# Eight experts of a mixture layer: plain fp32 products on four column groups in place of high and low parts

## What is computed

```python
def moe_swiglu(h, w_router, b_router, w_gate, w_up, w_down):
    logits = (ht @ w_router) + b_router                  # 256 x 8
    top_val, top_idx = lax.top_k(logits, TOP_K)          # 2 of 8
    gates = jax.nn.softmax(top_val, axis=-1)
    combine = jnp.sum(jax.nn.one_hot(top_idx, N_EXPERTS) * gates[..., None], axis=1)
    for e in range(N_EXPERTS):
        y = y + combine[:, e:e + 1] * swiglu(ht, w_gate[e], w_up[e], w_down[e])
```

## Time and profile before

| what | value |
|---|---|
| median of 3 runs | 1327.01 us |
| span of the profiled execution | 1322.7 us |
| around the span (median less span) | 4.3 us |
| PE busy | 1273.1 us, 96% |
| PEld busy | 889.4 us, 67% |
| DVE busy | 739.7 us, 56% |
| ACT busy | 625.3 us, 47% |
| moved by DMA | 422.91 MB |

### The profile page before, as it was taken

How to read it: one execution, slowest core, us unless ns; L and a number is a source line. 1 busy time by engine, 2 the same in 40 slices (tenths; PEclk the granted TensorE clock), 3 DMA queues, 4 the chain that set the end, 5 groups by cost and what they waited for, 6 DMA issues and landing times.

```text
span 1322.7 us, 15779 instructions
## 1 busy us (share of the span) xinstructions
PE 1273.1 (96%) x6168; PEld 889.4 (67%) x6169; DVE 739.7 (56%) x920; ACT 625.3 (47%) x722; POOL 39.0 (3%) x48
## 2 busy tenths in 40 slices
PE   7988999999998989999999999999999999999997
PEld 6765788888756778375847565856656775747572
DVE  5877554453466467374727465636646643837460
ACT  5575553353348537173526354525444533626450
POOL 1012000000003100000000000000000000000000
PEclk9999999999998989999999999999999999999999
DMA  9632455364352659899999999999999999999996
GB/s 344 224 127 96 150 183 187 119 229 145 115 199 89 244 228 354 305 388 414 421 422 420 420 417 418 421 421 422 420 418 418 421 420 421 421 419 417 420 421 250
DMA packets 88755, 422.91 MB, mean 320 GB/s; under 512 B 8560, under 2 KB 15462, under 8 KB 57958
## 3 DMA queue, kind: packets, MB, share of 16 engines
q1 hardware_dynamic: 87468, 419.10, 80.2%
q0 software_dynamic: 992, 2.69, 0.6%
q10 hardware_dynamic: 218, 0.08, 0.0%
HBM read 420.77 MB, written 1.07 MB: 319 GB/s over the span
## 4 chain that ended last, share of the span: by engine, by line
PE 86%; DVE 5%; DMA 4%; ACT 3%; issue 1%; SPq 0%; DVEq 0%; ACTq 0%
PE PS L2192 14%; PE PS L2172 11%; PE PS L2167 11%; PE PS L2168 11%; PE PS L1706 7%; PE PS L1710 7%; PE PS L1707 7%; PE PS L2184 6%; DMA raw<-in_w_down_o_dram 3%; PE PS L2029 2%; PE PS L2199 1%; PE PS L2107 1%; DVE w_r L977 1%; PE PS L2116 1%; ACT w_r L504 1%
## 5 line engine op out<-in xcount | busy, mean ns | idle before, releaser
L1387 DVE TENSOR_TENSOR w_r<-raw,w_r 128x2048 fp32r<-128x2048 f32 (+1 forms) x143 | 299.6, 2097 | 188.7 <-ACT w_r L806 188.1
L806 ACT ACTIVATE w_r<-raw 128x2048 fp32r<-128x2048 f32 (+1 forms) x143 | 251.9, 1762 | 194.5 <-PE PS L2168 124.1
L2167 PE MATMUL PS<-w_r,a_hi 128*128 128x512 f32 x512 | 201.6, 394 | 0.0
L2168 PE MATMUL PS<-w_r,a_lo 128*128 128x512 f32 x512 | 199.9, 390 | 0.0
L2192 PE MATMUL PS<-raw,xs 128*64 128x512 f32 (+1 forms) x792 | 157.7, 543 | 0.0
L977 DVE TENSOR_TENSOR w_r<-raw,w_r 128x2048 fp32r<-128x2048 f32 (+4 forms) x61 | 129.1, 2143 | 42.7 <-ACT w_r L504 42.5
L1706 PE MATMUL PS<-w_r,a_hi 128*128 128x512 f32 (+4 forms) x384 | 144.4, 380 | 6.0 <-DVE a_lo L1006 5.0
L1707 PE MATMUL PS<-w_r,a_lo 128*128 128x512 f32 (+4 forms) x384 | 141.8, 373 | 0.0
L2167 PEld LDWEIGHTS PS<-w_r,a_hi 128*128 128x128 f32 x512 | 96.2, 188 | 27.5 <-issue 8.0
L504 ACT ACTIVATE w_r<-raw 128x2048 fp32r<-128x2048 f32 (+4 forms) x61 | 106.6, 1800 | 15.3 <-PE PS L1710 12.6
L2192 PEld LDWEIGHTS PS<-raw,xs 128*64 128x64 f32 x792 | 54.1, 137 | 84.3 <-issue 76.1
(11 more groups left out here) (321 smaller groups left out, 1445.5 us busy)
## 6 DMA issues: line engine op xcount, KB each, us to landing
raw<-in_w_down_o_dram SPq DMA_DIRECT2D x88, 1024.0 KB, 20.3
raw<-in_w_up_o_dram SPq DMA_DIRECT2D x49, 1024.0 KB, 18.9
raw<-in_w_gate_o_dram SPq DMA_DIRECT2D x48, 1024.0 KB, 16.3
raw<-in_w_gate_o_dram SPq DMA_DIRECT2D x51, 768.0 KB, 13.3
raw<-in_w_up_o_dram SPq DMA_DIRECT2D x50, 768.0 KB, 12.7
slots<-in_w_down_o_dram SPq DMA_DIRECT2D x24, 1024.0 KB, 21.3
slots<-in_w_gate_o_dram SPq DMA_DIRECT2D x15, 1024.0 KB, 14.9
raw<-in_w_in_e_dram SPq DMA_DIRECT2D x12, 1024.0 KB, 10.4
```

What stands on the lines that cost most here:

```text
L806: nc.scalar.activation(w_r[:, high_slot(g), 0:w], place_of(n)[:, 0:w], ACT.Copy).then_inc(hi_done, 1)
L1387: nc.vector.tensor_tensor(place_r(n)[:, 0:w], place_of(n)[:, 0:w], w_r[:, high_slot(g), 0:w], ALU.subtract).then_inc(lo_done, 1)
L2167: nc.tensor.matmul(PS[:, bank, :], xh(x), hi[:, c0:c0 + NT], start=first, stop=False)
L2168: ins = nc.tensor.matmul(PS[:, bank, :], xl(x), hi[:, c0:c0 + NT], start=False, stop=False)
```

## The change

All experts take the way of the small ones, and in 32-token tiles:

- A product has 32 slots of tokens as stationary and a quarter of the chunk's columns as moving operand, and four of them go to the four column groups (PSUM partitions 0, 32, 64, 96). A large expert has 3 tiles (96 slots), a small one 2 (64 slots). No high and low parts are made: `esplit` on ACT and DVE, `large_low`, and the low parts of the gathered tokens and of the result are gone.
- The quarters are 512 columns in T=0, 384 in T=1, 256 in a down chunk.
- The order of a pair is large T=0, large T=1 (k 0 to 31), small T=0, small T=1 (32 to 63), large down, small down. So the first 32 chunks belong to expert 0, and only chunk 32 on waits for the order.
- 17 places (the two high slots and a part of `a_lo` are places now), 3 once places, 20 early loads.
- The large result is brought back inside its pair (k=82) with 24 products of 256 columns, the small one with 16; each has 32 rows of slots as contraction, in four row groups. The gates are in the return picks themselves. The gather of a pair is one set of 16 products (8 blocks x 2 token halves) of 160 columns. DVE adds four pieces of two token halves x 256 columns, for the large and for the small expert apart.
- The six last down chunks of an expert take their rows in another pattern (`DOWN_THIRDS`); two of them read 4 KB at a time where the others read 8 KB.
- The store at the end is by 256 columns of both token halves.

```diff
-E_RAW, E_HI, E_FIRST = 14, 2, 16
+E_RAW, E_FIRST = 17, 20
+Q = P // 4
+L_TILES, S_TILES = 3, 2
+L_CAP, S_CAP = L_TILES * Q, S_TILES * Q
...
-            return k // 16 % 2 == 1, "gu"[k // 8 % 2], k // 32, k % 8
+            return k >= GATE_UP, "gu"[k // 8 % 2], k // 16 % 2, k % 8
...
-            for n in (4, 5, 13, 14, 15):
+            for n in (4, 5, 13, 14):
                 expert_chunk(0, n, 0)
-            for n in range(6, 12):
-                ring_chunk(n)
+            for slot, n in enumerate((6, 7, 8, 9, 10, 11, 12, 15, 16)):
+                ring_chunk(n, slot + 4)
+                if n == 15:
+                    expert_chunk(0, 17, 0)
+            sp.wait_ge(sem("hn_set"), 2)
+            sp.wait_ge(sem("norm_ss"), 16)
+            expert_chunk(0, 19, 0)
             sp.wait_ge(mm_done, C_ROUTE + 1)
-            expert_chunk(0, 12, 0)
+            expert_chunk(0, 18, 0)
+            for n in range(E_FIRST, GATE_UP):
+                expert_chunk(0, n, 0)
             sp.wait_ge(sem("order_set"), 1)
-            pair_weights(0, 16, 0, order_of(PAIRS))
+            pair_weights(0, GATE_UP, 0, order_of(PAIRS))
...
+            def expert_products(p, k):
...
+                pe.wait_ge(*landed(n))
+                if kind == "d":
+                    for kk in range(2):
+                        f = down_block(at, kk)
+                        for j in range(tiles):
+                            for g in range(4):
+                                ins = nc.tensor.matmul(PS[g * Q:(g + 1) * Q, banks[j], 0:YC], acts[:, f, j * Q:(j + 1) * Q],
+                                                       w[:, kk * D + g * YC:kk * D + (g + 1) * YC], ...)
+                else:
+                    for j in range(tiles):
+                        for g in range(4):
+                            ins = nc.tensor.matmul(PS[g * Q:(g + 1) * Q, banks[j], 0:c], xe[:, at, x0 + j * Q:x0 + (j + 1) * Q],
+                                                   w[:, g * c:(g + 1) * c], start=at == 0, stop=at == DC - 1)
                 ins.then_inc(mm_done, 1)
...
+            def bring_back(of, y, tiles, banks):
+                for t in range(TT):
+                    for j in range(tiles):
+                        for g in range(4):
+                            rows_g = slice(g * Q, (g + 1) * Q)
+                            ins = nc.tensor.matmul(PS[:, banks[g], t * YC:(t + 1) * YC], of[rows_g, j, t * P:(t + 1) * P],
+                                                   y[rows_g, j, :], start=j == 0, stop=j == tiles - 1)
```

More of the change, by code:

```diff
@@ L136, in hybrid_trunk @@
         rs = sb("rs", [P, 2 * NH, 4])
[L137 to L140, removed]
+        pos = sb("pos", [P, TT, NE + SPARES])
+        comb = sb("comb", [P, TT, SPARES])
+        need = sb("need", [1, SPARES + 1], i32)
+        order = sb("order", [1, SPARES], i32)
         ident = cst[:, K_ID:K_ID + P]
@@ L260, in hybrid_trunk @@
                 freed[hi_slot(c)] = c + 1
-        HIGH0 = hi_slot(C_OUTO)
-        E_SLOTS = sorted((s for s in freed if s not in range(HIGH0, HIGH0 + E_HI)), key=lambda s: (freed[s], s))
-        assert len(E_SLOTS) == E_RAW - 3
+        E_SLOTS = sorted(freed, key=lambda s: (freed[s], s))
+        assert len(E_SLOTS) == E_RAW - 4
         RING = [raw[:, s, :] for s in E_SLOTS]
[L268 to L274, removed]
+        RING[4:4] = [slots[:, 0, :]]
+        RING += [a_lo_slot[:, :], slots[:, 1, :], slots[:, 2, :]]
+        ONCE = {5: once_g[:, 0, :], 13: once[:, 0, :], 14: once[:, 1, :]}
         AT_FIRST = [n for n in range(E_FIRST) if n not in ONCE]
@@ new lines, in gather_first @@
+            def gather_first():
+                pe.wait_ge(sem("moe_pick"), 1)
+                for h in range(2):
+                    for d in range(4):
+                        dc = 4 * h + d
+                        for t in range(TT):
+                            ins = nc.tensor.matmul(PS[:, GATHER[h], d * L_CAP:(d + 1) * L_CAP], xn[:, t, dc * P:(dc + 1) * P],
+                                                   xpick[:, t, 0:L_CAP], start=t == 0, stop=t == 1)
+                    ins.then_inc(sem("moe_gath"), 1)
@@ new lines, in gather @@
+            def gather(p):
+                pe.wait_ge(sem("moe_pick"), p + 2)
+                for i, (a, b) in enumerate(GATHERED):
+                    for dc in range(a, b):
+                        for t in range(TT):
+                            ins = nc.tensor.matmul(PS[:, GATHER[i], (dc - a) * X_CAP:(dc - a + 1) * X_CAP],
+                                                   xn[:, t, dc * P:(dc + 1) * P], xpick[:, t, :], start=t == 0, stop=t == 1)
+                    ins.then_inc(sem("moe_gath"), 1)
@@ new lines, in expert_products, with block_columns, turn_large @@
+                ins.then_inc(mm_done, 1)
+            def block_columns(block, T, b):
+                if T == 0:
+                    return two_rows(block, b)
+                return block[:, 0:E_COLS[1]].rearrange("p (r k) -> p k r", k=3)[:, b, :]
+            def turn_large(p, T, j):
+                pe.wait_ge(sem("l_mul"), 6 * p + 3 * T + j + 1)
+                for b in range(E_BLOCKS[T]):
+                    ins = nc.tensor.transpose(PS[:, LARGE_UP[T][j], b * P:(b + 1) * P], block_columns(sg_l[:, j, :], T, b), ident)
@@ L2307, in spare @@
             def spare(i):
-                gather(i, 4, "spare_pick", "spare_gath")
+                spare_gather(i)
                 pe.wait_ge(sem("spare_xlo"), 2 * i + 2)
```

628 lines of the change are left out of this document (288 added, 340 removed).

## The result

The kernel after takes 1333.37 us (median of 5 runs, 1331.81 to 1335.46), the kernel before 1327.06 (1325.73 to 1328.34) beside it: ratio 1.0045, interval 1.0034 to 1.0057. It is 0.45% slower, where 1316 us was forecast. The profiled execution took 1335.46 us, its span is 1333.6.

The account below looks back on a forecast made before the run. DMA was taken as the bound: 1271.1 floor plus 25.6 pauses, 2.3 landing and 1.8 last chunk gave 1300.8, taken as 1301; 10.5 for the end and 4.3 around the span made 1315.8, forecast 1316 us, range 1308 to 1356.

Parts of the forecast that it names:

- Overlap of four groups, PE's work per pair: Expert products: four column groups overlap in full plus 2.6 ns a record, 204.1 us of PE per pair.
- Bringing back: Returning a pair's expert results: 40 products of 256 columns, 5.5 us, between 4.3 and 8.8.
- Rival B: Expert products: 2400 records a pair for 1000 come too densely, PE slower, 1337 to 2035 us; chance 0.28.
- the lost fifth: Expert products: a fifth of the column groups' overlap lost, 20 ns on each record, 1502 us.
- Who sets the pace: End of the experts: DMA's chain at 1300.8 is later than PE's alone at 1295.6.
- DMA's floor and its last byte: Loads from 442.3: 348.1 MB at 420 GB/s end at 1271.1, with 25.6 of pauses 1296.7; 11 of 36 us won.
- Pauses up to 560 us: DMA pauses at the experts' start: 3.4, 16.7 and 1.5 us, plus 4 for few loads outstanding, 25.6 in all.
- Rival A: Early phase stays as it is: DMA pauses 30 us, bringing back costs its upper bound, 1322 to 1326 us; chance 0.14.
- The start: Fifth early load at 442.3 us, taken from the kernel before as the start of DMA's sum.
- The end: From last product to end of span: 9.7 us before, 10.5 after, for narrower copy, later pieces and shorter store rows.
- Around the span: Time outside the profiled span: 4.3 us, as between the present span and the median of 1327.0.

Follow-up runs that it names:

- the table: Kernels before, after, after with small experts in 64-slot tiles, with most small or all experts' products cut: half-rate stretch 4.6 to 14 us, 1.4 to 1.5 us per packet.
- its twin with shifted places: 32 bytes of padding put ahead of the arena in the kernel before: 1328.48 us, ratio 1.0009.
- the threshold of DVE's code: DVE memsets added per expert chunk to the kernel after: 5 (14 more packets) 1333.65 us, 14 (41 more) 1355.18, 28 (82 more) 1393.29.
- the last run: Kernel after with large experts' 0.79 MB chunks first and small experts alone in one 64-wide tile on two column groups: 1327.44 us, ratio 0.9998.

## Why the prediction was wrong

The profiled execution took 1335.46 us where 1316 was forecast: 19.5 us. By the prediction's own steps:

- **Overlap of four groups, PE's work per pair: right.** 109.5 and 55.8 ns a record for 109.3 and 55.9. Bringing back 2.87 + 2.01 = 4.9 us for 5.5. PE, freed, is busy 190 to 194 of 200 us. Rival B, which held 0.28, did not come. The Trainium skill (TensorE: Matmul & The Clock Gate, "Wait — 56ns, not 53.3ns?" and "Measured speedup vs the span model") has two figures that stood for it. The first, 62 ns a product, it gives for hardware decode off, and a record of 256 columns at 55.8 ns shows that it doesn't bind here. The second is 2.38 times for three column groups; four gave 427 / 109.5 = 3.9 times here, so the lost fifth was not seen.
- **Who sets the pace: right.** DMA's chain, as the waits at the end show.
- **DMA's floor and its last byte: the step that failed.** I treated the 16 engines as one pipe of 420 GB/s and put the transfers of PE's code at nothing, without a reason: the page of the kernel before has their queue, and rival B counts 2400 records for 1000. I counted what lay between that and the last landing before (36 us) as pauses. From 560 us on, 348.1 - 382 x 41.31 / 1000 - 278 x 71.36 / 1000 = 312.5 MB were left; at 420 GB/s they end at 1304.0, and with the 2.3 us of landing PE's last chunk would start at 1306.3. It starts at 1320.64: 14.3 us lost. 3.6 are the rate (418 for 420), and 10.7 lie behind it. They are better read as one thing: the early eight engines end at 1303, where the floor of 420 has its end (1304.0), and the late eight some 14 us after. Eight engines that fall 14 us behind on the way also lower the sum, and the full stretches show it faintly: 420 GB/s with 31 packets, 419 with 58 and 63, 418 or 419 with 77. Before, the same sum (442.26 on; 316 and 307 GB/s up to 560, so 311.6 MB left, 1301.9 + 2.3) gives 1304.2. PE starts its last two chunks at 1309.31 and the second of them 1.85 us later: 6.9 us lost, 2.7 of them in a pause between 560 and 700 (412 GB/s), 4.2 behind it. These 4.2 us I had booked as a pause that the change could win; the change made them 13.6. 46 more packets of code, 46 / 8 x 1.5 = 8.6 us by the table, are most of the difference.
- **Pauses up to 560 us: right in size.** (420 - 382) / 420 x 41.31 + (420 - 278) / 420 x 71.36 = 27.9 us, forecast 25.6. But the pauses before were smaller than 36: by the same sum 9.9 + 20.9 to 560, and 2.7 up to 700. So 33.5 became 28.6 (0.7 of it behind 560): 4.9 us won, where I had counted 11. Rival A had 30 us of pauses for my 25.6; the 27.9 measured lie midway.
- **The start: 5.1 us late**, the first early load behind the attention at 447.33, not 442.26. The program is the same up to there. In the 18 profiled executions (all kernels here share it) this issue lies between 442.26 and 449.91, and the kernel before has the earliest of all and its twin with shifted places 446.84; so most of the 5 us belongs to the one execution from which I read, and not to the change.
- **The end: right.** 1333.6 less 1322.57 (1320.64 + 1.93) is 11.0, forecast 10.5.
- **Around the span: 2.4 us too much.** I took 4.3 us, a median less the span of another execution; the runs have 1.9 (1335.46 - 1333.6).

5.1 + 2.3 (pauses, 27.9 for 25.6) + 14.3 + 0.5 - 2.4 = 19.8, for 19.5 measured. Without the start, which is scatter, and the slip around the span, about 17 us of error stand, 14.3 of them the late end of the loads.

So the change wins 4.9 us of pauses, loses 13.6 - 4.2 = 9.4 to late engines and slower pace, and 1.3 in its last steps (11.0 for 9.7). That makes 5.8 us, which is the difference of the two spans (10.9) without the start (5.1); the medians differ by 6.3. Of the 9.4, the code's 8.6 are worked out from the lags; the rest is not assigned, and rows of 4 KB are not told from scatter. That the eight late engines are those which bring PE's code is an inference, since the trace names no engine for a packet; it rests on the lags that go with the packets in every kernel of the table, on the threshold of DVE's code, and on the last run. No run moved the code to other engines or left it out with the records kept. The Trainium skill (Runtime: NRT & Kernel Launch, "Instruction fetch mechanics") says of a 16 KiB block of code that crossing its boundary is "mostly hidden". For PE that holds here: no wait of PE for code is seen. For the transfers it doesn't, at 1.5 us on one engine.

## What to carry to other kernels

In a kernel bound by transfers, look at how the last loads end: a stretch at half (or a sixteenth) of the bandwidth points to engines that were late all along, and that lag, not the mean GB/s, sets the time. Instructions then have a price even where their own engine has time to spare: here 1.5 us per 256 of PE's on one of eight DMA engines, so 0.19 us at the end of the loads, and 0.9 us per 128 of DVE's on one engine alone, with nothing to pay until that one is later than the others. And what separates the floor from the measured end must be split into its causes before a change is credited with it.

## What was not expected of the hardware

- The code of DVE seems to come through one DMA engine (25 GB/s alone for 18 us at the end), that of PE over eight (200 to 256 GB/s for 14 us). 82 packets of DVE's code, 8 KB each, cost 60 us.
- 24 chunks with two DMAs of eight partitions each added 145 us.
- A change between column tiles of 64 and of 32 slots costs PE some 0.14 us, where the records of tiles of one size follow each other with a surplus of 2.5 to 2.8 ns.
